# Reordering the ends of two mixers: turned row sums behind the last gate unit, high parts ahead of a sigmoid and of a row copy

## The chip, the cores and the metric

The kernel runs on one core of a Trainium2 chip. The metric is the device time of one execution in microseconds; medians of several executions are given.

## What is computed

Two transformer-like blocks over one sequence of 512 tokens, 1024 features wide, in 32-bit floats. The first block has a gated feed-forward part, a token mixer and a second feed-forward part. The token mixer joins an mLSTM (4 heads) and an HGRN (4 heads). The second block has a gated linear attention mixer (GLA), an MLP, a differential attention mixer and an MLP. Two ends of mixers matter here:

```python
# token_mix
hm = merge_heads(mlstm_chunkwise(q, k, v, log_i, log_f))      # divides by max(|den|, exp(-m_t))
out_m = head_rmsnorm(hm, mnorm_g, MLSTM_HEADS) * jax.nn.sigmoid(mo)
out_h = head_rmsnorm(ho, hnorm_g, HGRN_HEADS) * jax.nn.silu(hg)
return jnp.concatenate([out_m, out_h], axis=-1) @ w_out
# gla_mixer
o = rmsnorm_2(o, norm_g).reshape(B, T, D_MODEL)               # per head of 256 features
return (o * jax.nn.silu(r + b_r)) @ w_o
```

## The kernel before

Activations lie with features on the 128 partitions and the 512 tokens along the free dimension, as 8 feature tiles. A weight **unit** is 128x1024 numbers: 128 output features, 8 feature tiles of input. Products are split in three for precision: a number is a high part (a rounded copy) and a low part (the rest), and a product is high x high, low x high and high x low. So each unit is loaded into `raw` (6 slots, filled by the SP queue, which waits until VectorE has used the slot), ScalarE copies it to `whi` (L1013), VectorE subtracts to get `wlo` (L1611), and TensorE does 24 products (L289 to L291) of 128x512. `prep_to(n)` in the ScalarE and VectorE programs issues these copies and subtractions up to unit n. `unit(tag)` calls it for the unit three ahead (`NW - 1`) and is the first call in every step that handles a unit, in `gate()` too.

The five engines have programs of their own, written out in order (`Pe`, `Act`, `Dve`, `Pool`, `Sp`). Each engine does its instructions in that order and waits on semaphores where `w.wait_ge` stands. Banks are the 8 PSUM banks, taken in turn.

**End of the first mixer.** The last eight units before the output projection are gates, `hg` (4) and `mo` (4). In `Pe.mix` `gate()` is one unit by `linear`, which can call a `hook` ahead of its third feature tile. The head outputs of the mLSTM are squared, summed over the features by products with ones (`rows`, L515), copied out of PSUM by ScalarE (`rows_out`, L1134), and turned into columns by four small products (`turned_rows`, L524). The last gate unit has the turning of ("m",) as its hook. From the columns and from the denominators (`den`) comes a reciprocal root: `Abs` on ScalarE (L1371), four small VectorE steps (`dden` 0 to 3, L2137 to L2144), `Sqrt` on ScalarE (L1373), reciprocal on VectorE (L1671). TensorE spreads it over the partitions in 4 x 4 products (`mR`, L557), VectorE multiplies the heads by it (L2152), ScalarE makes the high parts (`to_y`, L1228), VectorE the low ones (L1967). The output projection `wout` begins with two units in a `pair`: first all high parts (L403, L404), in the order of heads 4 to 7 (HGRN) and then 0 to 3 (mLSTM), with the spreads between, and then all low parts (L408). The heads 4 to 7 need nothing of the mLSTM: their high parts wait only for the last gate unit, since they overwrite its input. A gate is a sigmoid or SiLU on ScalarE (L1335), a product with the norm's weight on VectorE (L2107) and, for `mo`, a product with the head output on GpSimd (L2430).

**End of the GLA mixer.** Eight value products `mv` 0 to 7 (L651, L654) are squared by ScalarE (L1049) and multiplied with the gates by VectorE (L2223). Heads 0 and 1 (tiles 0 to 3, half 0) are summed, turned and rooted during the later value products; heads 2 and 3 (half 1) after them. `heads_normed(0)` in `Pe.gla` spreads both roots of half 0 after `mv` 6; then come `mv` 7, the row sums of half 1 (`half_rows(1)`) and the pair of `go` units, which has the turning ahead of its feature tile 2 and the spreads of half 1 ahead of tile 4. ScalarE, after the last square, copies the rows of half 1 (L1134) and then makes the high parts of tiles 0 to 3. VectorE multiplies tiles 0 to 3 by the spread root (L2215) and makes their low parts before it takes `mv` 7.

Of the kernel before, what the change touches and what calls it, by code (L numbers as in the profile page):

```python
# [9 lines left out]
S = 512  # L10
# [24 lines left out]
    ("diff_subln_g_2", 1), ("final_g_2", 8), ("mlstm_gate_b", 1), ("diff_lambda_2", 256),  # L35
]

IDENT, ONES, PERM, CAUS, CNEG, INVF_C, EPS_C, HPI_C, SEL_C, QUAD_C, PAIR_C, NCONST = 0, 128, 256, 384, 512, 640, 641, 642, 643, 647, 655, 679

QUADRANTS = ("mif", "ga")  # L40
MIX_ORDER = [("hq", 0, 4), ("mif", 0, 1), ("hf", 0, 4), ("hi", 0, 4)]
# [217 lines left out]
class Pe(Engine):  # L259
# [5 lines left out]
            self.w.wait_ge(*self.sig.on(self.sig.emptied[before][0], *self.sig.emptied[before][1]))  # L265
        return tile

    def linear(self, tag, x, order=range(8), kts=None, hook=None):


        w, sig, e, k = self.w, self.sig, self.e, self.k
        xh, xl, lo, st = x
        u = self.count(tag)
        out = self.bank("u", u)
        w.wait_ge(*sig.on("wlo", u))
        order = list(order if kts is None else range(kts))
        for kt in order:
            if hook and kt == order[2]:
                hook()
            w.wait_ge(*sig.on(lo, *st, kt))  # L280
            self.three(out, u, kt, xh[:, kt, :], xl[:, kt, :], kt == order[0], kt == order[-1])
        return u
# [375 lines left out]
    def mix(self):  # L658
        w, sig, e, k = self.w, self.sig, self.e, self.k
        y = (k.yhi, k.ylo, "ylo", ("mix",))  # L660
# [36 lines left out]
        heads = k.ident[:, 0:128:32]  # L697
# [35 lines left out]
                                  start=j == 0, stop=j == 3)  # L733
            mm.then_inc(*(sig.up("rows", "den") if pair else sig.up("mden")))

        def gate(hook=None):
            self.linear("hg" if self.k.lin[self.u][2] == "hg" else "mo", y, hook=hook)

        weights(0)
        weights(1)  # L740
# [4 lines left out]
        scored(0)  # L745
        weights(2)
        gate()
        scored(1)
        weights(3)
# [19 lines left out]
        self.turned_rows(("den",), k.tm(0)[:, 0:S], heads, ("den",))  # L769
        w.wait_ge(*sig.on("hsq", "m", 3))  # L770
        self.rows(("m",), range(4, 8))
        gate(lambda: self.turned_rows(("m",), k.tm(1)[:, 0:S], heads, ("mrow",)))

        def mlstm_spreads():
            w.wait_ge(*sig.on("hroot", "m"))
# [3 lines left out]
        x = (k.yhi, k.ylo, "ylo", ("mixx",))  # L779
        order = [4, 5, 6, 7, 0, 1, 2, 3]  # L780
# [5 lines left out]
    def gla(self):  # L786
        w, sig, e, k = self.w, self.sig, self.e, self.k
        y = (k.yhi, k.ylo, "ylo", ("gla",))
        self.four(["gq"] * 4, y, "yhi", 3, 2)
        self.quadrants("ga", "gla")  # L790
        for i in range(4):
            self.linear("gk", y)
            out = self.bank("gz", i)
            w.wait_ge(k.s_a2, 16)
            w.wait_ge(*sig.on("galr"))
            e.matmul(out, k.tm(0)[:, 128 * i:128 * i + 128], k.tm(1)[:, 0:S], start=True,
                     stop=True).then_inc(*sig.up("gz", i))
        for _ in range(2):
            self.tokens("gv", y)
        todo = deque(range(8))  # L800

        def bg():
            if todo:
                todo.popleft()
                self.linear("gr", y)

        self.decay("gla", k.gq, k.gk, bg)
        while todo:
            bg()
        pairs = k.cst[:, PAIR_C:PAIR_C + 2]  # L810

        def heads_normed(half):
            w.wait_ge(*sig.on("hroot", "g", half))
            for h in (2 * half, 2 * half + 1):
                self.spread(("gR", h), k.hs[half], h % 2, 2)

        def half_rows(half):
            w.wait_ge(*sig.on("hsq", "g", 4 * half + 3))
            self.rows(("g", half), range(0, 4) if half else range(4, 8))

        def half_turned(half):
            self.turned_rows(("g", half), k.tm(6 if half else 7)[:, 0:S], pairs, ("grow", half))

        w.wait_ge(*sig.on("vals", "g", 7))
        for i in range(8):
            self.mix_values("gla", i, i // 2, k.gvals, 128 * i)
            if i == 4:
                half_rows(0)
            if i == 5:
                half_turned(0)  # L830
            if i == 6:
                heads_normed(0)
        half_rows(1)

        def second(kt):
            if kt == 2:
                half_turned(1)
            if kt == 4:
                heads_normed(1)

        x = (k.yhi, k.ylo, "ylo", ("glax",))
        self.pair(["go", "go"], x, "yhi", hook=second)
        for _ in range(6 - HALVED["gla"]):
            self.linear("go", x)
        self.last_units("gla", "go", lambda kt: (k.yhi[:, kt, :], k.ylo[:, kt, :]), ("ylo", "glax"), HALVED["gla"])
# [147 lines left out]
class Act(Engine):  # L993
# [255 lines left out]
    def mix(self):  # L1249
        k, w, sig, e, F = self.k, self.w, self.sig, self.e, self.k.ACT  # L1250
# [79 lines left out]
        def gate():  # L1330
            i = gates.popleft()
            u = self.unit("mo" if i < 4 else "hg")
            w.wait_ge(*sig.on("lin", u))
            dst = k.mo[:, i, :] if i < 4 else k.hg[:, i - 4, :]
            e.activation(dst, k.banks.at("u", u), F.Sigmoid if i < 4 else F.Silu).then_inc(  # L1335
                *sig.up("gact", i, bank=("u", u)))
# [24 lines left out]
        outputs(3)  # L1361
        self.rows_out(("den",), 0)
        gate()
        self.rows_out(("m",), 1)
        gate()
        w.wait_ge(*sig.on("lin", k.last["mo"]))
        for h in range(4):
            self.to_y("mixx", 4 + h, k.hq[:, h, :], "hn", "h", h)
        d = k.hs[1]
        w.wait_ge(*sig.on("hcol", "den"))  # L1370
        e.activation(d, k.banks.at("den")[:, 0:16], F.Abs).then_inc(*sig.up("dabs", bank=("den",)))  # L1371
        w.wait_ge(*sig.on("dden", 3))
        e.activation(d, d, F.Sqrt).then_inc(*sig.up("dabs", "sqrt"))  # L1373

# [4 lines left out]
        us = self.pair(["wout", "wout"], mlstm_normed)  # L1379
# [9 lines left out]
    def gla(self):  # L1389
        k, w, sig, e, F = self.k, self.w, self.sig, self.e, self.k.ACT  # L1390
# [44 lines left out]
        def row_root(half):  # L1435
            w.wait_ge(*sig.on("hcol", "g", half))
            self.columns_root("hrsq", ("g", half), k.hs[half], 8, ("grow", half))

        def heads_normed(half):
            w.wait_ge(*sig.on("lin", k.last["gr"]))  # L1440
            for i in range(4 * half, 4 * half + 4):
                self.to_y("glax", i, k.rg[:, i, :], "hn", "g", i)

        for i in range(8):
            w.wait_ge(*sig.on("mixv", "gla", i))
            self.square("hsq", ("g", i), k.tm(4 + i if i < 4 else i - 4)[:, 0:S], k.banks.at("mv", "gla", i))
            if i == 2:
                self.ready_root()
            if i == 4:
                self.rows_out(("g", 0), 7)  # L1450
            if i == 5:
                row_root(0)
        self.rows_out(("g", 1), 6)
        heads_normed(0)
        row_root(1)
        us = self.pair(["go", "go"], lambda: heads_normed(1))
        for n in range(NT - HALVED["gla"]):
            if n >= 2:
                self.unit("go")
# [128 lines left out]
class Dve(Engine):  # L1588
# [419 lines left out]
    def mix(self):  # L2008
        k, w, sig, e, ALU = self.k, self.w, self.sig, self.e, self.k.ALU
# [119 lines left out]
        gate()  # L2129
        gate()  # L2130
        gate()
        for h in range(4):
            self.to_y("mixx", 4 + h, k.hq[:, h, :])
        d, em = k.hs[1], k.hs[2]
        w.wait_ge(*sig.on("dabs"))
        w.wait_ge(*sig.on("gem"))
# [6 lines left out]
        w.wait_ge(*sig.on("hcol", "m"))  # L2143
        e.scalar_tensor_tensor(d, k.banks.at("mrow")[:, 0:16], 1 / 128, d, ALU.mult, ALU.add).then_inc(  # L2144
            *sig.up("dden", 3, bank=("mrow",)))
        self.columns_root("hroot", ("m",), k.hs[1], "dabs", "sqrt")

        def mlstm_normed():
# [8 lines left out]
        us = self.pair(["wout", "wout"], mlstm_normed)  # L2157
# [9 lines left out]
    def gla(self):  # L2167
        k, w, sig, e, ALU = self.k, self.w, self.sig, self.e, self.k.ALU
# [38 lines left out]
        while todo:  # L2207
            bg()

        def heads_normed(half):  # L2210
            for h in (2 * half, 2 * half + 1):
                w.wait_ge(*sig.on("spread", "gR", h))
                for i in (2 * h, 2 * h + 1):
                    w.wait_ge(*sig.on("gg", i))
                    e.tensor_tensor(k.rg[:, i, :], k.rg[:, i, :], k.banks.at("gR", h), ALU.mult).then_inc(  # L2215
                        *sig.up("hn", "g", i, bank=("gR", h) if i % 2 else None))
            for i in range(4 * half, 4 * half + 4):
                self.to_y("glax", i, k.rg[:, i, :])

        for i in range(8):  # L2220
            w.wait_ge(*sig.on("hsq", "g", i))
            w.wait_ge(*sig.on("grg", i))
            e.tensor_tensor(k.rg[:, i, :], k.rg[:, i, :], k.banks.at("mv", "gla", i), ALU.mult).then_inc(  # L2223
                *sig.up("gg", i, bank=("mv", "gla", i)))
            if i == 5:
                self.columns_root("hroot", ("g", 0), k.hs[0][:, 0:8], "hrsq", "g", 0)
            if i == 6:
                heads_normed(0)
        self.columns_root("hroot", ("g", 1), k.hs[1][:, 0:8], "hrsq", "g", 1)
        us = self.pair(["go", "go"], lambda: heads_normed(1))  # L2230
        for n in range(NT - HALVED["gla"]):
            self.gated("gla", 0, n, us[n] if n < 2 else self.unit("go"), 11)

# [512 lines left out]
```

## Time and profile before

| what | us |
| --- | --- |
| median of 3 runs | 2377.09 |
| lowest and highest | 2372.65, 2377.21 |
| the profiled execution | 2377.69 |
| its span, first to last instruction | 2375.9 |
| TensorE busy in the span | 2320.1 (98%) |
| VectorE busy | 1336.7 (56%) |
| ScalarE busy | 846.4 (36%) |
| GpSimd busy | 210.3 (9%) |
| mean granted TensorE clock | 0.986 of full speed |

All times of the trace are microseconds from the start of the span. The first mixer ends at about 706, the GLA mixer's gate products at about 1316. PE is TensorE, ACT ScalarE, DVE VectorE, POOL GpSimd. The profile reports an instruction's start and its length; instructions of one engine overlap in part, so the pitch of equal instructions is shorter than their length.

### The profile page before, as it was taken

To read this page: it belongs to the slowest core of one execution; us is meant where nothing else is said; L and a number is where in the kernel's file an instruction comes from. 1 tells how busy PE (TensorE), PEld (TensorE's weight loads), DVE (VectorE), ACT (ScalarE), POOL (GpSimd) and SP (SyncE) were. 2 spreads that over 40 slices of the span, in tenths; PEclk is the share of its full clock that TensorE was granted. 3 is DMA by queue.
4 is the path that set the end of the run, shared out by engine and by line. 5 is a ranking of instruction groups with operands and counts; after the bars stand their busy time and mean duration, and the time that the engine had idled before them with its cause. 6 is when DMAs were issued, how large, how long until landed. Compare 5 with 4: busy or idle time off the path is not lost.

```text
span 2375.9 us, 27396 instructions
## 1 busy us (share of the span) xinstructions
PE 2320.1 (98%) x11040; PEld 1895.9 (80%) x11040; DVE 1336.7 (56%) x1985; ACT 846.4 (36%) x1286; POOL 210.3 (9%) x177
## 2 busy tenths in 40 slices
PE   8999999999999999999999999999999989999998
PEld 7888888777778888887787988888877768888887
DVE  7654547586348454548543566664466665644343
ACT  3322223423434322223733442322344454423221
POOL 0000003021014000003110100000121101000001
PEclk8999999999999999999999999999999999999999
DMA  7766642311212366542231256663131112443331
GB/s 311 247 207 195 197 122 65 108 44 45 71 54 62 116 215 207 190 125 72 76 98 54 72 172 218 210 198 115 46 110 54 54 45 63 154 121 96 90 98 36
DMA packets 81918, 286.99 MB, mean 121 GB/s; under 512 B 9089, under 2 KB 11521, under 8 KB 81793
## 3 DMA queue, kind: packets, MB, share of 16 engines
q1 hardware_dynamic: 80928, 283.41, 37.4%
q8 instruction: 88, 1.44, 0.3%
q10 hardware_dynamic: 864, 1.84, 0.2%
q14 instruction: 38, 0.30, 0.0%
HBM read 283.11 MB, written 2.10 MB: 120 GB/s over the span
## 4 chain that ended last, share of the span: by engine, by line
PE 86%; DVE 9%; ACT 3%; issue 1%; POOL 1%; DMA 0%; SPq 0%; DVEq 0%; ACTq 0%; POOLq 0%
PE bank L289 23%; PE bank L291 23%; PE bank L290 23%; DVE wlo L1611 2%; PE bank L506 1%; PE bank L452 1%; PE bank L426 1%; PE bank L447 1%; PE bank L428 1%; PE bank L427 1%; PE bank L448 1%; PE bank L557 1%; ACT whi L1013 1%; DVE attd L1991 1%; DVE dsm L2301 1%
## 5 line engine op out<-in xcount | busy, mean ns | idle before, releaser
L1611 DVE TENSOR_TENSOR wlo<-raw,whi 128x1024 fp32r<-128x1024 f32 (+1 forms) x368 | 473.1, 1287 | 331.8 <-ACT whi L1013 331.4
L289 PE MATMUL bank<-yhi,whi 128*128 128x512 f32 (+1 forms) x1670 | 656.3, 393 | 0.5 <-DVE ylo L1967 0.5
L291 PE MATMUL bank<-yhi,wlo 128*128 128x512 f32 (+1 forms) x1670 | 645.2, 386 | 0.0
L290 PE MATMUL bank<-ylo,whi 128*128 128x512 f32 (+1 forms) x1670 | 645.2, 386 | 0.0
L1013 ACT ACTIVATE whi<-raw 128x1024 fp32r<-128x1024 f32 (+1 forms) x368 | 383.1, 1042 | 303.4 <-PE bank L291 256.9
L289 PEld LDWEIGHTS bank<-yhi,whi 128*128 128x128 f32 x1670 | 314.4, 188 | 82.3 <-issue 19.5
L291 PEld LDWEIGHTS bank<-yhi,wlo 128*128 128x128 f32 x1670 | 314.3, 188 | 64.1
L290 PEld LDWEIGHTS bank<-ylo,whi 128*128 128x128 f32 x1670 | 314.6, 188 | 61.5 <-issue 1.4
L289 PE MATMUL bank<-mlp_ahi,whi 128*128 128x512 f32 (+1 forms) x552 | 209.3, 379 | 0.0
L291 PE MATMUL bank<-mlp_ahi,wlo 128*128 128x512 f32 (+1 forms) x552 | 209.0, 379 | 0.0
L290 PE MATMUL bank<-mlp_alo,whi 128*128 128x512 f32 (+1 forms) x552 | 208.9, 378 | 0.0
L1628 DVE SCALAR_TENSOR_TENSOR raw<-raw,crow 128x1024 f32<-128x1024 f32 x152 | 183.7, 1218 | 0.0
L1908 DVE SCALAR_TENSOR_TENSOR h_sb<-bank,mod,h_sb 128x512 f32<-128x512 f32 (+1 forms) x91 | 62.1, 685 | 183.2 <-PE bank L291 183.2
L1194 ACT ACTIVATE tmps<-bank 128x512 f32<-128x512 f32 x108 | 64.4, 597 | 263.0 <-PE bank L291 263.0
L291 PE MATMUL bank<-ffn_ahi,wlo 128*128 128x512 f32 x352 | 139.0, 395 | 0.0
L289 PE MATMUL bank<-ffn_ahi,whi 128*128 128x512 f32 x352 | 139.0, 395 | 0.0
L290 PE MATMUL bank<-ffn_alo,whi 128*128 128x512 f32 x352 | 139.0, 395 | 0.0
L290 PEld LDWEIGHTS bank<-mlp_alo,whi 128*128 128x128 f32 x552 | 103.7, 188 | 21.7
L289 PEld LDWEIGHTS bank<-mlp_ahi,whi 128*128 128x128 f32 x552 | 103.7, 188 | 21.5
L291 PEld LDWEIGHTS bank<-mlp_ahi,wlo 128*128 128x128 f32 x552 | 103.7, 188 | 21.5
L2389 POOL TENSOR_TENSOR tmps<-tmps 128x512 f32<-128x512 f32 x36 | 54.3, 1529 | 737.5 <-ACT tmps L1049 737.5
L1200 ACT ACTIVATE ffn_ahi<-tmps 128x512 fp32r<-128x512 f32 x44 | 27.8, 632 | 189.6 <-DVE tmps L1928 189.6
(347 smaller groups left out, 2849.4 us busy)
## 6 DMA issues: line engine op xcount, KB each, us to landing
raw<-in_ada SPq DMA_DIRECT2D x152, 512.0 KB, 4.4
raw<-in_ffn_up SPq DMA_DIRECT2D x88, 512.0 KB, 4.4
raw<-in_mlp_up SPq DMA_DIRECT2D x64, 512.0 KB, 3.6
raw<-in_mlp_dn SPq DMA_DIRECT2D x64, 512.0 KB, 3.6
raw<-in_ffn_dn SPq DMA_DIRECT2D x32, 512.0 KB, 4.0
raw<-in_w_dqkv SPq DMA_DIRECT2D x24, 512.0 KB, 3.6
first<-in_ada SPq DMA_DIRECT2D x16, 512.0 KB, 14.5
raw<-in_ffn_dn SPq DMA_DIRECT2D x16, 384.0 KB, 3.4
```

What stands on the lines that cost most here:

```text
L289: e.matmul(out, wh, xh, start=first, stop=False)
L290: e.matmul(out, wh, xl, start=False, stop=False)
L291: mm = e.matmul(out, wl, xh, start=False, stop=last)
L426: e.matmul(outs[j], xh[:, kt, t], wh, start=kt == 0, stop=False)
L427: e.matmul(outs[j], xl[:, kt, t], wh, start=False, stop=False)
L1013: self.e.activation(k.whi[:, n % NW, 0:width], k.raw[:, slot, 0:width], k.ACT.Copy).then_inc(*self.sig.up("whi", n))
L1194: e.activation(buf, k.banks.at("u", u), fn).then_inc(*sig.up("hid", st, g, i, bank=("u", u)))
L1200: e.activation(k.ahi[st][g % 2][:, i, :], buf, k.ACT.Copy).then_inc(*sig.up("ahi", st, g, i))
L1611: e.tensor_tensor(k.wlo[:, what % NW, 0:width], raw[:, 0:width], k.f(k.whi[:, what % NW, 0:width]), ALU.subtract).then_inc(*sig.up("wlo", ...
L1628: self.e.scalar_tensor_tensor(raw, raw, 1.0, k.crow[:, :], k.ALU.mult, k.ALU.mult, accum_out=k.mod[:, at:at + 1]).then_inc(*sig.up("ada", ...
L1908: self.e.scalar_tensor_tensor(h, y, k.mod[:, 8 * v_gate + n:8 * v_gate + n + 1], h, k.ALU.mult, k.ALU.add).then_inc(*self.sig.up("acc", st ...
L2389: self.e.tensor_tensor(acc, acc, k.tm(total + 1)[:, 0:S], ALU.add).then_inc(*sig.up(kind + "add", st, n))
```

## The change

Each part is an order of instructions; no work is added or left out.

- In the first mixer the four turning products of ("m",) go from inside the last gate unit to behind it; the `hook` of `linear` goes.
- On ScalarE `Abs` goes ahead of the copy of the rows, and the last `gate()` goes from ahead of the four high parts of heads 4 to 7 to between the second and the third.
- On VectorE the four low parts of heads 4 to 7 go from ahead of the four `dden` steps to behind them.
- In GLA one of the two spreads of half 0 goes from ahead of `mv` 7 to behind it, and so do VectorE's products with it and the four low parts of half 0. On ScalarE the high parts of tiles 0 and 1 go ahead of the copy of the rows of half 1.
- The table of constants is 711 instead of 679 columns long; the new ones are zero and not read.

```diff
-IDENT, ONES, ..., QUAD_C, PAIR_C, NCONST = 0, 128, ..., 647, 655, 679
+IDENT, ONES, ..., QUAD_C, PAIR_C, NCONST = 0, 128, ..., 647, 655, 711
# Pe.mix
-        gate(lambda: self.turned_rows(("m",), k.tm(1)[:, 0:S], heads, ("mrow",)))
+        gate()
+        self.turned_rows(("m",), k.tm(1)[:, 0:S], heads, ("mrow",))
# Pe.gla
-            if i == 6:
-                heads_normed(0)
+            if i >= 6:
+                head_normed(i - 6)
         half_rows(1)
# Act.mix
         outputs(3)
         self.rows_out(("den",), 0)
         gate()
-        self.rows_out(("m",), 1)
-        gate()
-        w.wait_ge(*sig.on("lin", k.last["mo"]))
-        for h in range(4):
-            self.to_y("mixx", 4 + h, k.hq[:, h, :], "hn", "h", h)
         d = k.hs[1]
         w.wait_ge(*sig.on("hcol", "den"))
         e.activation(d, k.banks.at("den")[:, 0:16], F.Abs).then_inc(*sig.up("dabs", bank=("den",)))
+        self.rows_out(("m",), 1)
+        w.wait_ge(*sig.on("lin", k.last["mo"]))
+        for h in range(4):
+            if h == 2:
+                gate()
+            self.to_y("mixx", 4 + h, k.hq[:, h, :], "hn", "h", h)
         w.wait_ge(*sig.on("dden", 3))
         e.activation(d, d, F.Sqrt).then_inc(*sig.up("dabs", "sqrt"))
# Act.gla
+        heads_normed(0, 2)
         self.rows_out(("g", 1), 6)
-        heads_normed(0)
+        heads_normed(2, 4)
         row_root(1)
-        us = self.pair(["go", "go"], lambda: heads_normed(1))
+        us = self.pair(["go", "go"], lambda: heads_normed(4, 8))
# Dve.mix
         gate()
         gate()
         gate()
-        for h in range(4):
-            self.to_y("mixx", 4 + h, k.hq[:, h, :])
         ...
         e.scalar_tensor_tensor(d, k.banks.at("mrow")[:, 0:16], 1 / 128, d, ALU.mult, ALU.add).then_inc(
             *sig.up("dden", 3, bank=("mrow",)))
+        for h in range(4):
+            self.to_y("mixx", 4 + h, k.hq[:, h, :])
         self.columns_root("hroot", ("m",), k.hs[1], "dabs", "sqrt")
# Dve.gla
-            if i == 6:
-                heads_normed(0)
+            if i >= 6:
+                head_normed(i - 6)
+        half_low(0)
         self.columns_root("hroot", ("g", 1), k.hs[1][:, 0:8], "hrsq", "g", 1)
-        us = self.pair(["go", "go"], lambda: heads_normed(1))
+        us = self.pair(["go", "go"], second)
```

## Rows read from the trace of the kernel before

**Rows 1.** Page, chain that ended last: share of the span by engine

```profile
PE 86%; DVE 9%; ACT 3%; issue 1%; POOL 1%; DMA 0%; SPq 0%; DVEq 0%; ACTq 0%; POOLq 0%
```

**Rows 2.** Timeline, TensorE, first mixer's end: start, length, line, count, [idle before <-releaser]

```profile
684.21 0.95 PE L524 MATMUL bank<-cst,tmps 128*128 128x4 f32 x8
685.02 0.49 PE L289 MATMUL bank<-yhi,whi 128*128 128x512 f32 x1
...
690.81 0.47 PE L403 MATMUL bank<-yhi,whi 128*128 128x512 f32 x1 [1.41 <-ACT yhi L1228]
...
695.49 3.84 PE L557 MATMUL bank<-cst,hs 128*128 128x128 f32 x32 [0.77 <-DVE hs L1671]
```

**Rows 3.** Timeline, ScalarE, first mixer's end

```profile
683.35 1.05 ACT L1013 ACTIVATE whi<-raw 128x1024 fp32r<-128x1024 f32 x1
689.44 0.60 ACT L1335 ACTIVATE hf<-bank 128x512 f32<-128x512 f32 x1 [5.04 <-PE bank L291]
689.94 2.18 ACT L1228 ACTIVATE yhi<-hq 128x512 fp32r<-128x512 f32 x4
...
692.21 1.28 ACT L1373 ACT_TABLE_LOAD   x1
694.94 0.21 ACT L1373 ACTIVATE hs<-hs 128x16 f32<-128x16 f32 x1 [1.45 <-DVE hs L2144]
```

**Rows 4.** Timeline, VectorE, first mixer's end

```profile
690.07 0.49 DVE L2107 TENSOR_SCALAR hf<-hf,par 128x512 f32<-128x512 f32 x1 [3.47 <-ACT hf L1335]
690.59 3.60 DVE L1967 TENSOR_TENSOR ylo<-hq,yhi 128x512 fp32r<-128x512 f32 x4
...
695.18 0.25 DVE L1671 RECIPROCAL hs<-hs 128x16 f32<-128x16 f32 x1 [0.28 <-ACT hs L1373]
696.13 1.22 DVE L1611 TENSOR_TENSOR wlo<-raw,whi 128x1024 fp32r<-128x1024 f32 x1 [0.69 <-ACT whi L1013]
```

**Rows 5.** Timeline, GpSimd, first mixer's end

```profile
690.64 1.80 POOL L2430 TENSOR_TENSOR hf<-hf,mqk 128x512 f32<-128x512 f32 x1 [2.89 <-DVE hf L2107]
```

**Rows 6.** Timeline, TensorE, end of the GLA mixer

```profile
1297.57 1.95 PE L557 MATMUL bank<-cst,hs 128*128 128x128 f32 x16
1299.35 0.39 PE L651 MATMUL bank<-gattd,gvals 128*128 128x128 f32 x2
...
1302.40 1.06 PE L515 MATMUL bank<-tmps,cst 128*32 128x512 f32 x8 [0.69 <-ACT tmps L1049]
1304.74 0.47 PE L403 MATMUL bank<-yhi,whi 128*128 128x512 f32 x1 [1.28 <-issue]
...
1309.43 1.95 PE L557 MATMUL bank<-cst,hs 128*128 128x128 f32 x16
1311.93 0.50 PE L403 MATMUL bank<-yhi,whi 128*128 128x512 f32 x1 [0.55 <-ACT yhi L1228]
```

**Rows 7.** Timeline, ScalarE, end of the GLA mixer

```profile
1301.75 0.60 ACT L1049 ACTIVATE tmps<-bank 128x512 f32<-128x512 f32 x1 [3.38 <-PE bank L651]
1303.53 0.60 ACT L1134 ACTIVATE tmps<-bank 128x512 f32<-128x512 f32 x1 [1.19 <-PE bank L515]
1304.02 2.18 ACT L1228 ACTIVATE yhi<-grg 128x512 fp32r<-128x512 f32 x4
```

**Rows 8.** Timeline, VectorE, end of the GLA mixer

```profile
1308.91 1.22 DVE L1611 TENSOR_TENSOR wlo<-raw,whi 128x1024 fp32r<-128x1024 f32 x1 [0.74 <-ACT whi L1013]
```

**Rows 9.** Windows of 2 us: length, TensorE busy (instructions), granted clock, DMA, GB/s

```profile
1302.00:1304.00 2.00, 1.06 (x8) 1.00 0.00 0
...
1854.00:1856.00 2.00, 0.67 (x5) 0.90 0.60 219
1856.00:1858.00 2.00, 2.00 (x6) 0.50 0.00 0
1858.00:1860.00 2.00, 2.00 (x10) 0.75 0.00 0
```

**Rows 10.** DMA issues: count, KB each, us to landing

```profile
cst<-in_cst SPq DMA_DIRECT2D x1, 339.5 KB, 5.2
```

More of the change, by code:

```diff
@@ L36 @@
 ]
-IDENT, ONES, PERM, CAUS, CNEG, INVF_C, EPS_C, HPI_C, SEL_C, QUAD_C, PAIR_C, NCONST = 0, 128, 256, 384, 512, 640, 641, 642, 643, 647, 655, 679
+IDENT, ONES, PERM, CAUS, CNEG, INVF_C, EPS_C, HPI_C, SEL_C, QUAD_C, PAIR_C, NCONST = 0, 128, 256, 384, 512, 640, 641, 642, 643, 647, 655, 711
 QUADRANTS = ("mif", "ga")
@@ L266, in bank, with linear @@
         return tile
-    def linear(self, tag, x, order=range(8), kts=None, hook=None):
+    def linear(self, tag, x, order=range(8), kts=None):
         w, sig, e, k = self.w, self.sig, self.e, self.k
@@ L277, in linear @@
         for kt in order:
-            if hook and kt == order[2]:
-                hook()
             w.wait_ge(*sig.on(lo, *st, kt))
@@ L734, in denominators, with gate @@
             mm.then_inc(*(sig.up("rows", "den") if pair else sig.up("mden")))
-        def gate(hook=None):
-            self.linear("hg" if self.k.lin[self.u][2] == "hg" else "mo", y, hook=hook)
+        def gate():
+            self.linear("hg" if self.k.lin[self.u][2] == "hg" else "mo", y)
         weights(0)
@@ L810, in gla, with head_normed @@
         pairs = k.cst[:, PAIR_C:PAIR_C + 2]
[L812 to L815, printed above, removed]
+        def head_normed(h):
+            w.wait_ge(*sig.on("hroot", "g", h // 2))
+            self.spread(("gR", h), k.hs[h // 2], h % 2, 2)
         def half_rows(half):
@@ L838, in second @@
             if kt == 4:
-                heads_normed(1)
+                head_normed(2)
+                head_normed(3)
         x = (k.yhi, k.ylo, "ylo", ("glax",))
@@ L1437, in row_root, with heads_normed @@
             self.columns_root("hrsq", ("g", half), k.hs[half], 8, ("grow", half))
-        def heads_normed(half):
+        def heads_normed(a, b):
             w.wait_ge(*sig.on("lin", k.last["gr"]))
-            for i in range(4 * half, 4 * half + 4):
+            for i in range(a, b):
                 self.to_y("glax", i, k.rg[:, i, :], "hn", "g", i)
@@ L2208, in gla, with head_normed, half_low, second @@
             bg()
[L2210 to L2216, printed above, removed]
+        def head_normed(h):
+            w.wait_ge(*sig.on("spread", "gR", h))
+            for i in (2 * h, 2 * h + 1):
+                w.wait_ge(*sig.on("gg", i))
+                e.tensor_tensor(k.rg[:, i, :], k.rg[:, i, :], k.banks.at("gR", h), ALU.mult).then_inc(
+                    *sig.up("hn", "g", i, bank=("gR", h) if i % 2 else None))
+        def half_low(half):
             for i in range(4 * half, 4 * half + 4):
                 self.to_y("glax", i, k.rg[:, i, :])
+        def second():
+            head_normed(2)
+            head_normed(3)
+            half_low(1)
         for i in range(8):
```

## Prediction

> **What bounds the kernel now.** I read the chain of work that ended last first: TensorE carries 86% of it [rows 1], so an edit is worth what it does to TensorE's gaps. Then I read TensorE's timeline round the two mixer ends for those gaps, and at each gap the timelines of ScalarE, VectorE and GpSimd backwards from the instruction that ended it. At the end of the first mixer the reader is to see two gaps, 1.41 us before the first high product of `wout` and 0.77 us before the `mR` spreads [rows 2]. At the end of the GLA mixer there are 0.69 us before the row sums of the second half, 1.28 us before the first product of `go`, and one before its fifth feature tile [rows 6]. Whatever can be won is in these places: some 5 us of 2376, or 0.2%. About 0.2% is also what a measurement of this kernel can tell from no change.
>
> **First mixer, the turning.** Four turned products move from inside the last gate unit to behind it. Inside they cost 0.81 us (684.21 to 685.02), and the product behind them takes 0.49 us [rows 2], some 0.1 more than its neighbours: 0.9 us in all. Behind the unit they lie in the 1.41 us in which TensorE waits for the high part of head 4. So the unit ends 0.9 us earlier, at 688.5 instead of 689.4 on the clock of the trace, and the turning is hidden.
>
> **First mixer, ScalarE.** Before, the last sigmoid starts at 689.44 when the unit ends, then four high parts at a pitch of 0.52 us [rows 3]. After, two high parts come first (688.5 and 689.0), then the call `gate()`. That call doesn't only issue the sigmoid: its first line, `unit`, prepares the weight copy of the unit three ahead. Before, this copy (1.05 us) ran at 683.35, in ScalarE's idle time [rows 3], because `gate()` was entered early and waited inside. After, the queue stands at the wait for the last unit ahead of that call, so the copy runs at 689.6 and ends at 690.6. The sigmoid runs at 690.5 to 691.1, the last two high parts until 692.2. TensorE's first product can start at 689.4 instead of 690.8, but its third feature tile waits for a high part until 691.9.
>
> **First mixer, VectorE.** The weight's low part is made from that copy, and VectorE's `gate()` also prepares before it waits for the sigmoid. So a subtraction of 1.22 us (the length of one that runs alone) [rows 4] starts at 690.6, and the norm factor's product at 691.8. Before it started at 690.07 [rows 4]. That is 1.7 us later, the sum of two high parts 1.04, the copy 1.05 and the subtraction 1.14 (its pitch), less the 0.6 us from the sigmoid's start to the product and the 0.9 of the turning. From there the same instructions lie between product and reciprocal, only ordered otherwise: four small ones ahead of four low parts instead of behind. Before this took 5.11 us (690.07 to 695.18), of which the last 0.28 were a wait for the root [rows 4]. The root is now made while the low parts run: its table load of 1.28 us [rows 3] ends at 693.5, the fourth small step at the latest at 694.1. So it takes 4.83 us, and the reciprocal starts at 696.6 instead of 695.18: **1.4 us later**. All sixteen `mR` spreads wait for it.
>
> In the 5.11 us lies one collision: GpSimd's product (1.80 us) starts at 690.64 behind VectorE's [rows 5], and four low parts take 3.60 us instead of 4 times 0.62 [rows 4], 1.1 us more. After, the same GpSimd product starts beside the small steps; I keep the 1.1 us. If it met no VectorE instruction, the sum would be 0.3 instead of 1.4 us later; if every small step stood behind a whole product of its own it would be more, but there is only the one product. I take the row. The Trainium skill ("SBUF — State Buffer", section "SBUF: two separate sides") says that a VectorE instruction with two SBUF inputs and a GpSimd one exclude each other for a whole instruction. By it moving small steps ahead of the low parts moves the stall and doesn't remove it, 1.4 us; by a reading in which only long instructions collide it would be 0.3.
>
> **What is late next.** TensorE has done its four high feature tiles at 693.7 and then waits until 696.9 (690.81 to 694.5 before, and 0.77). The spreads took from 695.49 until 699.1 [rows 2], and the first normalized head is ready before they end; this stays. VectorE's next weight subtraction (1.22 us from 696.13 [rows 4]) is now covered by the first spread. The end of `wout`'s pair is thus 1.4 us later. The weight slot that the delayed subtraction gives back is wanted again six loads further, in the next stage, tens of us later: nothing. Moving `Abs` ahead of the row copy costs nothing: its columns are there before that copy's rows.
>
> **GLA mixer.** One of the two first spreads moves behind the last value product. Two spreads take 1.78 us (1297.57 to 1299.35) [rows 6], so that product ends 0.9 us earlier, its square starts at 1300.86 instead of 1301.75 and ends at 1301.5 [rows 7]. The second spread fills TensorE until just then: the 0.69 us gap goes, and the row sums start at 1301.5 instead of 1302.40. Before, the first high part followed the copy of the rows at 1304.02, 0.49 us behind 1303.53 [rows 7]. Now two high parts precede that copy; the first runs at 1301.4 to 1302.0, right behind the square, since VectorE has normalized its tiles by 1300.3. So `go` starts when the row sums leave TensorE, about 1.0 us behind their start (they are 1.06 us long [rows 6]), at 1302.5 instead of 1304.74: **2.2 us earlier**. The next tiles stay fed: the copy of the rows (1302.7 to 1303.3) is over before the turning at 1304.5, tiles 2 and 3 are high at 1303.8 and 1304.3. The second half's reciprocal is now behind four low parts, at 1305.9; its spreads are wanted at 1307.2. The weight subtraction (1.22 us, before at 1308.91) [rows 8] ends at 1307.9, ahead of the first spread at 1308.3. From the spreads on (1309.43 to 1311.93, [rows 6]) the chain of spread, product and high part is as it was, 2.2 us earlier.
>
> **Constants.** 32 columns more are 16 KB on a load of 339.5 KB that lands in 5.2 us [rows 10]; in proportion at most 0.25 us, and nothing where the tiles of x are later anyway. Later tensors lie 128 bytes further. No row shows a price for an address; I take 0 to 0.25, and 0.1.
>
> **Sum.** +1.4 - 2.2 + 0.1 = -0.7 us. The profiled execution took 2377.69 us (span 2375.9 and 1.8 around it), which gives 2377.0; it lies 0.6 above the median of 2377.09, so on the median it is **2376.4**.
>
> **Rivals.** (A) *The clock falls in the new gap.* TensorE would stand 3.2 us at 693.7 to 696.9, longer than any wait of the trace but the first load, and then do small spreads. At 1854 to 1856 TensorE was busy 0.67 of 2 us and the granted clock fell: 0.90, then 0.50, the lower of its two levels, 1.2 GHz, then 0.75 [rows 9]. At half speed were thus 0.4, 2.0 and 1.0 us of these three windows, 3.4 us. In the 2 us at that level 6 instructions ran, in the next 2 us 10. Against it: at 1302 to 1304 TensorE was busy 1.06 of 2 us and the clock stayed at 1.00 [rows 9], and so it stayed through the two gaps of the first mixer. A fall here would meet the spreads and the high parts, work that TensorE sets, so 3.4 us at half speed cost 1.7 us. It decides the sign: +1.0, **2378.1**; twice as long, +2.7, 2379.8. The skill's page "TensorE: Matmul & The Clock Gate" (section "HAM oscillation — how this bites in real kernels") warns of just this, that a wait between bursts brings the array back cold. The trace agrees at 1856. Chance 0.42, of this 0.12 for the longer one.
>
> (B) *The copy isn't late.* If the compiled order lets the weight copy run early, the product starts at 690.2 and the reciprocal at 695.0: first mixer -0.1, in all -2.2, **2374.9**. Against it speaks that one ScalarE queue runs in program order. The collision missing gives about as much (-1.8). Chance 0.08.
>
> (C) *The GLA part gives nothing*, as the next stage's weights or a bank of `gR` are late: the change then is only the 1.5 us of the first mixer, **2378.6**. Against it: each bank taken there was emptied before 1300. Chance 0.04.
>
> My forecast has 0.43; 0.03 remain for what I don't see.
>
> **Range and chances.** The shown runs alone span 2372.65 to 2377.21. I also allow for one stretch as in (A), 1.7 us, to come or go at another place, since the change shifts all behind 700 us. So from 2373.2 to 2380.0, which takes in (A) in both lengths, (B) and (C). Faster by over 0.2% means under 2372.3, slower means over 2381.8; no case reaches either without help from that scatter: 0.05 and 0.05, within 0.90.
>
> **What would show it.** Right: in ScalarE's timeline a weight copy of 1.05 us between the second high part and the last sigmoid; the `mR` spreads preceded by some 3 us of idle time; in GLA no idle time before the row sums and less than 0.2 us before `go`. Wrong: a spread that starts under 6.5 us behind the last gate unit; `go` starting over 1.5 us behind the row sums. The granted clock from 696 to 704 decides between forecast and (A).

## The result and the profile after

| | before | after |
| --- | --- | --- |
| median, us | 2376.24 (2372.65 to 2377.21, 4 runs) | 2362.39 (2361.1 to 2363.3, 4 runs) |
| profiled execution, its span | 2377.69, 2375.9 | 2361.83, 2360.0 |
| TensorE busy | 2320.1 (98%) | 2303.4 (98%) |

The changed kernel is faster: ratio 0.9941 [0.9925, 0.9956], where I had forecast 2376.4, in a range that begins at 2373.2. The gain isn't in either mixer end. It is in TensorE's busy time, 16.7 us less, for the same products.

The page's costliest groups, TensorE's alone, each with instructions, busy us and mean ns of one, and idle time before. First the kernel before:

```profile
L291 PE MATMUL bank<-yhi,wlo 128*128 128x512 f32 (+1 forms) x1670 | 645.2, 386 | 0.0
...
L289 PE MATMUL bank<-mlp_ahi,whi 128*128 128x512 f32 (+1 forms) x552 | 209.3, 379 | 0.0
```

Then the kernel after:

```profile
PE 2303.4 (98%) x11040; PEld 1897.2 (80%) x11040; DVE 1334.9 (57%) x1985; ACT 846.6 (36%) x1286; POOL 208.8 (9%) x177
...
L288 PE MATMUL bank<-yhi,wlo 128*128 128x512 f32 (+1 forms) x1670 | 645.5, 387 | 0.0
...
L286 PE MATMUL bank<-mlp_ahi,whi 128*128 128x512 f32 (+1 forms) x552 | 206.6, 374 | 0.0
```

Products that stream `yhi` are as they were. Those that stream `mlp_ahi`, the hidden activations of the MLP, lost 5 ns each. A length overlaps its neighbours', so what counts is the pitch, the time from one product's start to the next one's. It stands in TensorE's timeline, here in the second feed-forward part before:

```profile
1060.02 0.40 PE L291 MATMUL bank<-ffn_ahi,wlo 128*128 128x512 f32 x1
1060.25 0.39 PE L289 MATMUL bank<-ffn_ahi,whi 128*128 128x512 f32 x1
1060.48 0.40 PE L290 MATMUL bank<-ffn_alo,whi 128*128 128x512 f32 x1
1060.72 0.39 PE L291 MATMUL bank<-ffn_ahi,wlo 128*128 128x512 f32 x1
```

and after:

```profile
1059.73 0.39 PE L288 MATMUL bank<-ffn_ahi,wlo 128*128 128x512 f32 x1
1059.95 0.39 PE L286 MATMUL bank<-ffn_ahi,whi 128*128 128x512 f32 x1
1060.18 0.39 PE L287 MATMUL bank<-ffn_alo,whi 128*128 128x512 f32 x1
1060.41 0.39 PE L288 MATMUL bank<-ffn_ahi,wlo 128*128 128x512 f32 x1
```

Three products take 0.70 us before and 0.68 after. Over all such products the mean pitch is 233.3 ns before and 226.7 after; that of the `yhi` products is 227.2 in both kernels. There are 2472 of the hidden ones, 3 x 352 of `ffn` and 3 x 472 of `mlp` of the full 128x512, and 2472 x 6.65 ns = 16.4 us.

The same on TensorE's clock of starts, from the first to the last hidden product of each stage (products with `yhi` lie between them):

| stage | products | before | after |
| --- | --- | --- | --- |
| first feed-forward | 528 | 210.01 | 206.49 |
| second feed-forward | 528 | 210.01 | 206.49 |
| first MLP | 696 | 249.21 | 244.57 |
| second MLP | 720 | 254.82 | 250.01 |

Sum: -16.5 us. These four lengths repeat to 0.02 us in every trace of an equal layout below, while the stretches between them scatter by up to 3 us from one execution to the next; so the four lengths are the sharpest measure here.

Now the two ends that the prediction was about. TensorE at the end of the first mixer, where [rows 2] stood before:

```profile
681.01 0.95 PE L521 MATMUL bank<-cst,tmps 128*128 128x4 f32 x8
682.10 0.47 PE L400 MATMUL bank<-yhi,whi 128*128 128x512 f32 x1
...
684.37 0.50 PE L400 MATMUL bank<-yhi,whi 128*128 128x512 f32 x1 [0.17 <-ACT yhi L1226]
```

The gap of 1.41 us is gone; the turning lies in its place. ScalarE, as [rows 3]:

```profile
681.21 1.15 ACT L1226 ACTIVATE yhi<-hq 128x512 fp32r<-128x512 f32 x2 [5.06 <-PE bank L288]
682.27 1.05 ACT L1011 ACTIVATE whi<-raw 128x1024 fp32r<-128x1024 f32 x1
683.22 0.58 ACT L1333 ACTIVATE hf<-bank 128x512 f32<-128x512 f32 x1
```

VectorE, as [rows 4], and GpSimd's product, as [rows 5]:

```profile
683.35 1.23 DVE L1611 TENSOR_TENSOR wlo<-raw,whi 128x1024 fp32r<-128x1024 f32 x1 [8.48 <-ACT whi L1011]
684.49 0.48 DVE L2107 TENSOR_SCALAR hf<-hf,par 128x512 f32<-128x512 f32 x1
684.88 0.17 DVE L2135 TENSOR_TENSOR hs<-hs 128x16 f32<-128x16 f32 x1
685.09 1.28 DVE L2137 TENSOR_SCALAR hs<-hs 128x16 f32<-128x16 f32 x1
...
686.70 2.49 DVE L1967 TENSOR_TENSOR ylo<-hq,yhi 128x512 fp32r<-128x512 f32 x4
689.11 0.24 DVE L1671 RECIPROCAL hs<-hs 128x16 f32<-128x16 f32 x1
```

```profile
685.05 1.29 POOL L2437 TENSOR_TENSOR hf<-hf,mqk 128x512 f32<-128x512 f32 x1 [5.55 <-DVE hf L2107]
```

The weight copy comes between the second high part and the sigmoid, and its subtraction ahead of the norm's product. TensorE's windows of 2 us there (length, busy and count, granted clock, DMA, GB/s), of TensorE alone:

```profile
688.00:690.00 2.00, 0.59 (x4) 0.96 0.01 2
690.00:692.00 2.00, 2.00 (x12) 0.50 0.37 49
692.00:694.00 2.00, 2.00 (x14) 0.69 0.54 213
694.00:696.00 2.00, 2.00 (x14) 1.00 0.00 0
```

The clock fell to 0.50, its lower level of 1.2 GHz, about half a microsecond after the spreads had begun at 689.41, and those took 5.46 us instead of the 3.84 of [rows 2]. From the mLSTM's row sums to the end of `wout`'s pair: 24.73 us before, 27.57 after, of which the later start of the spreads is 1.2 (14.99 behind the row sums instead of 13.77) and the clock 1.6.

TensorE at the end of the GLA mixer, where [rows 6] stood:

```profile
1294.26 0.39 PE L648 MATMUL bank<-gattd,gvals 128*128 128x128 f32 x2
1294.49 1.06 PE L554 MATMUL bank<-cst,hs 128*128 128x128 f32 x8
1295.47 1.07 PE L512 MATMUL bank<-tmps,cst 128*32 128x512 f32 x8
1296.47 0.50 PE L400 MATMUL bank<-yhi,whi 128*128 128x512 f32 x1
...
1303.63 0.50 PE L400 MATMUL bank<-yhi,whi 128*128 128x512 f32 x1 [0.55 <-ACT yhi L1226]
```

No idle time ahead of the row sums (0.69 before), none ahead of `go` (1.28 before); the 0.55 us before the fifth tile stays. From GLA's first turning (half 0, at 1294.48 before and 1288.31 after) to the end of the pair of `go` it takes 22.70 us instead of 24.86.

So -16.5 + 1.2 + 1.6 - 2.2 = -15.9 us, which is the difference of the spans. That it comes out to the tenth is luck, since the stretches between scatter by more.

### The profile page after: what moved, and what is told of

It is laid out like the page before. It is cut to its first block, busy times and chain, and to the rows that moved or that the text cites. A ratio compares the mean times of both kernels' runs of the same rounds, so it can differ in the third digit from the quotient of the medians.

```text
span 2360.0 us, 27397 instructions
## 1 busy us (share of the span) xinstructions
PE 2303.4 (98%) x11040; PEld 1897.2 (80%) x11040; DVE 1334.9 (57%) x1985; ACT 846.6 (36%) x1286; POOL 208.8 (9%) x177
## 4 chain that ended last, share of the span: by engine, by line
PE 86%; DVE 9%; ACT 3%; issue 1%; POOL 1%; DMA 0%; SPq 0%; DVEq 0%; ACTq 0%; POOLq 0%
PE bank L286 23%; PE bank L288 23%; PE bank L287 23%; DVE wlo L1611 2%; PE bank L503 1%; PE bank L449 1%; PE bank L423 1%; PE bank L444 1%; PE bank L424 1%; PE bank L425 1%; PE bank L445 1%; PE bank L554 1%; ACT whi L1011 1%; DVE attd L1991 1%; PE bank L336 1%
```

## The experiments

Positions below count from the start of the mLSTM's row sums (first mixer) and from GLA's first turning; before has the spreads at +13.77, the pair's end at +24.73, and GLA's end at +24.86. The table at the end of this section has the lengths of the four stages.

**Which part of the change gives the gain? e1_const711**, the kernel before with the longer constants alone, and **e2_order679**, the kernel after without them.

```diff
-... NCONST = ..., 655, 679
+... NCONST = ..., 655, 711
```

> The kernel before with only the table of constants 711 instead of 679 columns long: every tensor allocated behind it, the hidden activations of the feed-forward parts (ffn_ahi, mlp_ahi and their low parts) among them, begins 128 bytes further; no instruction moves. Theory P (the pitch of a 128x512 product depends on where its moving operand begins): these products come at a pitch of 226.7 ns instead of 233.3, and 2472 of them save 16.4 us: about 2360. Rival R (the new order of the mixer ends did it, in a way not seen): no change, 2376. Rival S (the longer load of constants shifts the start of the weight stream): a change in the first 50 us alone.

> The changed kernel with the table of constants back at 679 columns: only the order of the mixer ends is changed. Theory P: products with ffn_ahi and mlp_ahi at 233.3 ns as before; what is left is +1.4 us in the first mixer, perhaps 1.6 more where TensorE's clock falls behind the 3 us gap, and -2.2 us in GLA: between -0.8 and +0.8 us, 2375.5 to 2377. Rival R: 2360 to 2362.

e1: 2360.34 us (2356.3 to 2363.79), ratio 0.9932 [0.9917, 0.9947]; both mixer ends as before (+24.70, +24.77). e2: 2376.97 (2372.76 to 2380.51), ratio 1.0002 [0.9993, 1.0012]. Thirty-two columns that nothing reads are the whole gain. They were the one part of the change that isn't an order of instructions. The reordering alone can't be told from no change, as I had forecast for the entire change. In e2 the spreads start at +14.97 and end the pair at +25.94, with the clock at 1.00 throughout, and GLA ends at +22.76. The windows of e2 round its gap:

```profile
690.00:692.00 2.00, 1.11 (x5) 0.56 (x3) 1.93 (x5) 1.31 (x3) 0.96 (x1) 1.00 0.80 238
692.00:694.00 2.00, 0.00 (x0) 0.00 (x0) 2.00 (x6) 0.61 (x1) 0.00 (x0) 1.00 0.06 25
694.00:696.00 2.00, 1.96 (x17) 1.97 (x18) 1.75 (x2) 0.05 (x1) 0.00 (x0) 1.00 0.00 0
```

(here all engines' busy times stand ahead of the clock, TensorE's first). TensorE idled 2.93 us, as long as in the kernel after, and no fall came.

**Length or address? e3_const743**: 64 columns more than before, 256 bytes.

> The kernel before with the table of constants 743 columns long: everything behind it begins 256 bytes further than before. Theory P with a period of 256 bytes: the hidden activations lie as before within 256 bytes, pitch 233.3 ns, no change (2376). With a period of 512 bytes or more: a pitch other than 233.3 ns, perhaps 226.7, and up to 16 us less.

2375.66 (2374.83 to 2378.63), ratio 0.9997 [0.9987, 1.0006]. The gain is gone: the longer load isn't what gave it. What matters is where the columns put the tensors behind them: within 256 bytes, these 64 leave them where they lay in the kernel before.

**Whose address? e4_pad_front**: 128 bytes ahead of all tensors of the kernel before.

```diff
+        sb("pad", [128, 32])
         k.h = sb("h_sb", [128, NT, S])
```

> The kernel before with an unused tensor of 128 bytes a partition ahead of all others: weights (whi, wlo), yhi, ylo and the hidden activations all begin 128 bytes further. Theory P (the start of the moving operand alone): the hidden activations come at 226.7 ns (-16 us), the some 5000 products with yhi and ylo at 233.3 (up to +33 us), in all up to 17 us slower. Rival T (it is where moving operand and weights lie to each other): as all move together, every pitch stays, 2376.

2375.21 (2373.51 to 2378.46), ratio 0.9998 [0.9988, 1.0007]. All tensors moved; `yhi` and the weights now start at a multiple of 256 bytes and the hidden tensors at 128 beyond one, where they lie in the kernel after, and they are slow all the same (pitch 233.3). So it isn't the absolute place of the streamed operand. What before, e3 and e4 have in common is the distance between `ahi` and the weights: 128 bytes beyond a multiple of 256. In e1 and after it is a multiple of 256.

**One tensor group alone: e9_pad_hidden**, the kernel before with a pad inside `hidden()`, ahead of the hidden tensors only.

```diff
+                sb(f"{st}_pad", [128, 32], fp32, s)
                 k.ahi[st] = [sb(f"{st}_ahi{i}", ...
```

> The kernel before with constants of 679 columns and an unused tensor of 128 bytes a partition ahead of the hidden activations of each feed-forward stage: these alone lie 128 bytes further, at distance 0 from the weights within 256 bytes; constants, scratch tiles and everything in the mixers keep their place. Theory T: pitch 226.7 ns, 16.4 us less, 2360 to 2361, as with the longer constants. Rival (another tensor moved by the constants does part of it): between 2361 and 2377.

2363.38 (2357.07 to 2365.65), ratio 0.9942 [0.9927, 0.9958]. The median lies in the rival's bounds, but the four runs are 8.6 us apart. The stages decide: all four have their fast lengths, to 0.01 us. Besides those tensors only `y`, in which a feed-forward stage adds up its output and which no product reads, has moved.

**Other distances: e5_four_offsets**, pads of 32, 64, 96 and 160 bytes ahead of the hidden tensors of the four stages, so that they lie 160, 192, 224 and 32 bytes beyond a multiple of 256 from the weights; and **e10_fine_offsets**, longer constants and hidden views that begin 4, 8, 16 and 256 bytes into their tensors.

```diff
-                k.ahi[st] = [sb(f"{st}_ahi{i}", [128, counts[i], S], f32r, s) ...
+                off = {"ffn1": 1, "ffn2": 2, "mlp0": 4, "mlp1": 64}[st]
+                    t = sb(name, [128, n * S + 64], f32r, s)
+                    return t[:, off:off + n * S].rearrange("p (n t) -> p n t", t=S)
```

> The kernel before with an unused tensor ahead of the hidden activations of each stage, so that they begin, against the weights and counted within 256 bytes, at -96 (ffn1, pad of 32 bytes a partition), -64 (ffn2, 64 bytes), -32 (mlp0, 96 bytes) and +32 bytes (mlp1, 160 bytes) instead of -128. The pitch of each stage's products is read. Theory T (distance to the weights within 256 bytes counts): if only the opposite half collides, -96 is slow (up to 233.3 ns) or in between and the small distances come at 226.7. If the distance must be exactly 0, all four come above 226.7. A pitch below 226.7 would mean that 0 isn't the best place.

> The kernel before with constants of 711 columns (distance 0), and the hidden activations beginning 4 bytes (ffn1), 8 bytes (ffn2), 16 bytes (mlp0) and 256 bytes (mlp1) into their tensors. Theory: 256 bytes are a whole period, pitch 226.7 ns. For 4, 8 and 16 bytes: if any distance within 256 bytes is slow, as -96 to +32 bytes were, 233.3 ns; if the addresses fall into blocks of 32 or 64 bytes or more, 226.7 ns for all three.

e5: 2377.49 (one run), all four stages slow. e10: 2374.08 (one run); mean pitch 238.0 ns at 4 bytes, 232.8 at 8, 231.7 at 16 and 226.7 at 256. The page's groups of e10:

```profile
L289 PE MATMUL bank<-mlp_ahi,whi 128*128 128x512 f32 (+1 forms) x552 | 207.5, 376 | 0.0
```

Its 376 ns, between the 379 of before and the 374 of after, is the mean of a slow first and a fast second MLP. So of the distances tried only a multiple of 256 bytes was fast. The others cost 5 to 8 ns a product, except 4 bytes, which cost 11.

**Which of the two weights? e6_wlo_apart**: 128 bytes between `whi` and `wlo` of the kernel before. `whi` is then right for `yhi` and for the hidden tensors, `wlo` wrong for both.

> The kernel before with an unused tensor of 128 bytes a partition between whi and wlo: whi keeps its place, wlo and all behind it begin 128 bytes further. The hidden activations then lie at distance 0 from whi and 128 from wlo; yhi and ylo, which don't move, are at 0 from whi and now at 128 from wlo. Theory T, with the collision between the streaming operand of one product and the loading of weights: of the three products of a feature tile, only those beside which wlo is loaded are slow, so that products with yhi too come at about 228.9 ns in the mean of three (680 + 6.7 ns) and those with hidden activations at 228.9 instead of 233.3. If only whi counts: 226.7 for both. If what counts is the place of wlo alone: 233.3 for both.

2390.12 (one run), some 12 us slower than before. Groups by shape:

```profile
L291 PE MATMUL bank<-yhi,wlo 128*128 128x512 f32 x1610 | 639.7, 397 | 0.0
...
L291 PE MATMUL bank<-ffn_ahi,wlo 128*128 128x512 f32 x352 | 139.8, 397 | 0.0
L290 PE MATMUL bank<-ffn_alo,whi 128*128 128x512 f32 x352 | 139.4, 396 | 0.0
L289 PE MATMUL bank<-ffn_ahi,whi 128*128 128x512 f32 x352 | 136.9, 389 | 0.0
```

The slowness has come to `yhi` too, the operand that was never slow (mean pitch 231.2 instead of 227.2). The hidden products came down to a mean of 231.1, where I had forecast 228.9. I had expected one slow step in three; two are slow. From start to start, the step from high x high (L289) to low x high (L290) is fast (226.7), the step from there to `wlo` (L291) takes 232.5 and the step from `wlo` to the next `whi` 234.2. In the trace the load of a product's weights starts some 3 ns behind the start of the product ahead of it. So the load of `wlo` goes on beside the stream of L290, 128 bytes off, and that step is slow as forecast. Beside the stream of L291 goes the load of the next `whi`, at distance zero, and that step is slow too. A distance from the loading weights alone doesn't explain it. Both slow steps are those in which the loaded weights change between `whi` and `wlo`, and their distance from each other is one more thing that only this run changed. Whether it has a part in the cost is untested. That the partner of the streamed tensor is the weights, and not another tensor that stayed put in e1, e9 and e10, rests on this run: `yhi` and `whi` didn't move, `wlo` did.

**GLA alone: e7_gla_only**, longer constants and the GLA part, the first mixer as before.

> The kernel before with the constants 711 columns long and the change in GLA; the first mixer's end as before. Theory: -16.4 us from the products with hidden activations, -2.2 us in GLA, and none of the first mixer's loss of 1.4 us and of the 1.6 us that the fallen clock cost there: 2357.8, 3 us below the changed kernel. Rival (the 3 us of the first mixer come back elsewhere, as another stretch at the lower clock): 2361 to 2362, as the changed kernel.

2358.29 (2355.82 to 2363.24), ratio 0.9922 [0.991, 0.9935]. The spreads at +13.74, the pair's end at +24.70, GLA's end at +22.70.

**The late copy: e8_copy_early**, the kernel after with the weight copy called for where ScalarE is idle.

```diff
         self.rows_out(("m",), 1)
+        self.prep_to(self.u + NW - 1)
```

> The changed kernel with one line more: ScalarE makes the weight copy of the unit three ahead before it waits for the last gate unit, and so does VectorE its low part. Theory (the copy and the subtraction behind it are what made the first mixer slower): the last sigmoid starts 1.0 us behind the unit's end, VectorE's product 1.7 us, the mR spreads some 1.5 us earlier than in the changed kernel, TensorE's gap ahead of them shrinks from 2.9 us to some 1.5 and the clock stays at its upper level: about 3 us below the changed kernel, 2359.3. Rival (the order of the high parts alone made it slower): spreads at the same distance from the unit's end, no change.

2359.79 (2357.47 to 2361.94), ratio 0.9926 [0.9913, 0.994]. The copy runs at 677.04, in idle time, and the spreads start at +13.39, 1.6 us earlier than in the kernel after:

```profile
688.80 3.84 PE L554 MATMUL bank<-cst,hs 128*128 128x128 f32 x32 [1.82 <-DVE hs L1672]
```

The gap is 1.82 us, the clock stays at 1.00, the pair ends at +24.37: 3.2 us less than after, half of it from the copy and half from the clock.

**The rest of the gap: e11_root_first**, e8 with VectorE's low parts of heads 4 to 7 behind the `mR` products, so that only the small steps stand ahead of the reciprocal.

```diff
-        for h in range(4):
-            self.to_y("mixx", 4 + h, k.hq[:, h, :])
         self.columns_root("hroot", ("m",), k.hs[1], "dabs", "sqrt")
...
+            for h in range(4):
+                self.to_y("mixx", 4 + h, k.hq[:, h, :])
```

> The changed kernel with the weight copy made early, and with VectorE's four low parts of heads 4 to 7 behind the products with the mR spreads instead of ahead of the reciprocal. Theory: the reciprocal follows the root at once, 11.2 us behind the row sums instead of 13.1, the spreads start 2.0 us earlier than with the copy early alone and TensorE's gap of 1.82 us ahead of them goes; the low parts are there at 693 and wanted at 694. The changed kernel's first mixer loses 5 us, and the whole takes 5.2 us less than the changed kernel: a ratio to it of 0.9978. Rival (the low parts are now late, or the collision with GpSimd moves to the path): the gap comes back ahead of the low products, and it takes as long as with the copy early alone.

2355.57 (2353.26 to 2357.05), ratio 0.9912 [0.9898, 0.9925], the fastest median of all. The reciprocal comes right behind the root, and the spreads right behind the high parts:

```profile
684.12 0.25 DVE L1672 RECIPROCAL hs<-hs 128x16 f32<-128x16 f32 x1 [0.28 <-ACT hs L1373]
```

```profile
684.26 0.39 PE L401 MATMUL bank<-yhi,wlo 128*128 128x512 f32 x1
684.49 3.78 PE L554 MATMUL bank<-cst,hs 128*128 128x128 f32 x32
```

They start at +11.41 and the pair ends at +22.95, 1.8 us less than before and 4.6 less than after. From the spreads to the end it takes 11.54 us instead of 10.96: the sixteen low products (L405) take 4.42 us instead of 3.79, as the low parts now come late. Against the kernel after on the same chip (e12 below) the medians are 7.6 us apart, a ratio of 0.9968 where I had expected 0.9978. The pair's end accounts for 4.6 of them; the other 3 lie in stretches that scatter and aren't explained.

**Is the fall of the clock in this place luck? e12_after_again**, the kernel after once more.

> The changed kernel as it is, on the same chip as the others of this call, to compare with. Both theories: the ratio of its first measurement, 0.994, with a stretch at the lower clock behind the 3 us gap of the first mixer in the trace if that fall is regular, without it if it depends on the moment.

2363.13 (2362.22 to 2367.38), ratio 0.9948 [0.9935, 0.996]. It fell again, at the same place behind a gap of 2.93 us, and the pair ended at +27.57 as in the first trace:

```profile
690.00:692.00 2.00, 0.50 (x4) 0.50 (x5) 2.00 (x5) 0.07 (x1) 0.00 (x0) 0.98 0.02 6
692.00:694.00 2.00, 2.00 (x11) 2.00 (x11) 1.21 (x2) 0.00 (x1) 0.00 (x0) 0.50 0.36 57
```

The four stages, from the first to the last hidden product, us, with the distance from the weights' start to the hidden tensors' start, in bytes beyond a multiple of 256:

| kernel | distance | FFN 1 | FFN 2 | MLP 1 | MLP 2 |
| --- | --- | --- | --- | --- | --- |
| before, e2, e3, e4 | 128 | 210.01 | 210.01 | 249.21 | 254.82 |
| after, e1, e7, e8, e9, e11, e12 | 0 | 206.49 | 206.49 | 244.57 | 250.01 |
| e5 | 160, 192, 224, 32 | 210.51 | 210.03 | 249.26 | 254.89 |
| e10 | 4, 8, 16, 0 | 212.48 | 209.76 | 248.10 | 250.01 |
| e6 | 0 to `whi`, 128 to `wlo` | 210.54 | 210.54 | 249.37 | 254.91 |

In e6 the lengths say little, since the `yhi` products between the hidden ones became slower while the hidden ones became faster.

## Why the prediction was wrong, step by step

**What bounds the kernel.** I read that TensorE carries 86% of the chain and then looked for gaps in it, "some 5 us of 2376". This was the first slip: with TensorE busy 98% of the span, a change of its pitch is worth more than all gaps, and I took the pitch for fixed. The profile had it in view. Two groups of the same shape differed (kernel before, groups by shape):

```profile
L291 PE MATMUL bank<-yhi,wlo 128*128 128x512 f32 x1610 | 628.3, 390 | 0.0
...
L291 PE MATMUL bank<-ffn_ahi,wlo 128*128 128x512 f32 x352 | 139.0, 395 | 0.0
```

5 ns apart in the mean of over 300 instructions, and nothing that an instruction says of itself explains it.

**Constants: the step that failed.** I wrote "Later tensors lie 128 bytes further. No row shows a price for an address; I take 0 to 0.25". The price was -16.5 us. The term was mis-sized, and its range left out that an address could give time back. An unseen cost is to be bounded from both sides, and the two groups above would have given the bound: if an address is what keeps the hidden products at 395 ns and `yhi` at 390, moving them can give 5 ns (by the pitches 233.3 and 227.2, 6 ns) on each of 2472, 12 to 15 us. The rest of the step held: the load lands in 5.0 us with 355.5 KB, against 5.2 in [rows 10].

**First mixer, the turning.** Right: the unit ends 0.9 us earlier, counted from the row sums, and the turning fills the wait behind it. The first product of `wout` starts 1.09 us behind the start of the turning (0.9 forecast), the third feature tile 3.36 behind it (3.4).

**First mixer, ScalarE and VectorE.** Right in order and nearly in size. From the unit's end: copy at 1.26 us (1.1 forecast), sigmoid 2.21 (2.0), subtraction 2.34 (2.1), product 3.48 (3.3), reciprocal 8.10 (8.1). That the last one agrees so well is partly luck: the product came 0.2 us later than forecast, and from there to the reciprocal it took 4.62 us instead of 4.83. Against before the spreads are 1.2 us later (1.4). e8 shows that the cause is the copy with its subtraction: moved alone it takes 1.6 us off.

**The collision.** Right: it moved. The second small step took 1.28 us beside GpSimd's product (1.29) while its like take 0.17, and the low parts fell from 3.60 [rows 4] to 2.49. The rule quoted from the Trainium skill ("SBUF — State Buffer", section "SBUF: two separate sides") agrees as far as the stall moved and stayed whole. But the step that was held has one SBUF input, not two; for such a step the same section asks that it run in a mode that uses both ports, and no run here shows in which mode it ran.

**What is late next, and rival A.** The gap is 2.92 us (3.2 forecast). The clock fell there and cost 1.6 us, as rival A said with +1.7 and a chance of 0.42. At half speed in after were 0.16, 2.0 and 1.2 us by the windows, 3.4 us, and half of that is 1.7. It came in both traces of after and not in e2, whose order is the same and whose gap is 2.93 us. At this place it came in none of the eleven traces whose gaps are shorter (1.82 us in e8). Elsewhere a shorter one was enough: in the kernel before the clock was down at 576, where TensorE had idled 1.52 us (kernel before, TensorE alone):

```profile
576.00:578.00 2.00, 1.17 (x3) 0.50 0.00 0
```

So the length of the gap doesn't decide alone. What does, these runs don't show.

**GLA.** Right: -2.16 against -2.2, and 22.70 in every kernel with this part (e7, e8, e11), 22.76 in e2. `go` starts 1.00 us behind the row sums. Rivals B and C didn't come about: the copy was late, and GLA gave its gain.

**Sum.** The two mixers and the load together: +1.2 - 2.2 = -1.0 without the fall, +0.6 with it; e2 measured 1.0002 [0.9993, 1.0012]. The forecast of "no change" was right for the mixers and the load, and wrong by the address, which I had put at next to nothing. The range was made of scatter and of rival A and held nothing for a change of pitch; that is why it was too narrow.

## What to carry to other kernels

Where TensorE is busy nearly all the time, compare the pitch of equal products by operand before looking at gaps, and look at it again after every edit that moves tensors. Ask whether the distance between the streamed operand and the weights is a multiple of 256 bytes per partition: here it was worth 16.5 us, four times what the best order of both mixer ends gave (1.8 and 2.2). Keep the layout fixed, or measure it apart, when the effect of an order is the question. A call that is moved takes its hidden first line with it, here a weight copy that cost 1.6 us; issue that part by itself where its engine is idle.

## What the runs showed of the hardware that I had not expected

- Products of 128x512 in fp32r run at a pitch of 226.7 ns when the streamed tensor and the weights start a multiple of 256 bytes apart in each partition, and at 231.7 to 238.0 when they don't (233.3 at 32, 128, 192 and 224 bytes, 234.3 at 160, 232.8 at 8, 231.7 at 16, 238.0 at 4). Moving all tensors by 128 bytes changed nothing (e4). The Trainium skill ("SBUF — State Buffer", section "SBUF: two separate sides") says that TensorE never waits on another engine's port. No run contradicts that, but the page gives no reason to expect a pitch that depends on the layout, and the measurement decides. That the streamed reads and the weight load, which go on at once, get in each other's way is my reading: it is argued from e6, where one of the two slow steps is the one beside the load of `wlo` and the other isn't explained, and not shown. Why almost every distance costs the same, and 4 bytes more, stays open. Other types weren't tried.
- The rule isn't one for every shape: the 240 hidden products of 128x256 in the MLPs went the other way, from a mean pitch of 120.1 ns at 128 bytes (before, e2, e3, e4) to 121.1 at a multiple of 256 (after, e1, e9).
- A small VectorE step on 16 columns took 1.1 us longer beside a GpSimd product of 512: 1.28 us in all five traces with this order (after, e2, e8, e11, e12), 0.17 in the nine with the old one, where the two ran apart.
- Equal gaps of 2.9 us were followed by a fall of the clock in two traces and by none in a third.
